# A two-layer diffusion step on one core: ten weight slots before the first expert choice, split constants, attention weights read early

## The chip, the core and the metric

The kernel runs on one NeuronCore of a Trainium2 chip. The metric is the device time of one execution in microseconds, as the median of several runs. In the text TensorE is PE, VectorE is DVE, ScalarE is ACT, GpSimd is POOL and SyncE is SP. SyncE does nothing but issue direct DMAs, in the order of its list; GpSimd issues the gathers.

## The reference, cut to what matters

Two groups of tokens (128 of a prompt, 512 of a sample) pass through two layers with shared weights. One layer, in float32 throughout:

```python
mod = silu(cond) @ w_ada[l] + b_ada[l]                 # shift1, scale1, gate1, shift2, scale2, gate2
h = rmsnorm(x, norm_mix) * (1 + scale1) + shift1
proj = h @ w_in[l]                                     # 3232 columns
hg = rmsnorm(scan_forward + scan_backward) * silu(gate)        # 8 heads, gated linear recurrence
ckv = rmsnorm(ckv_raw); k, v = ckv @ mla_wkvb[l]; q = rmsnorm(cq) @ mla_wqb[l]
attn = softmax(q k) v                                  # 8 heads; the sample also sees the cached context
x = x + gate1 * (concat(hg, attn) @ w_out[l])
h2 = rmsnorm(x, norm_ffn) * (1 + scale2) + shift2
q = h2 @ peer_wq[l]                                    # 2048 columns; scores against 2 x 128 keys per head
idx = top 16 of 16 x 16 candidates, for each of 8 heads       # 128 experts of 16384 per token
x = x + gate2 * sum(softmax(best) * gelu(h2 . u[idx]) * v[idx])
```

Outputs are the final norm of both groups and the prompt's new caches and scan states.

## The kernel before

The work is cut into four passes `p` = (group, layer): 0 is the prompt's first layer (one tile of 128 tokens), 1 the sample's first (four tiles), 2 and 3 the same for the second layer. Ten token tiles `u` = 0 to 9 in all need 128 gathers of `peer_u` rows and 128 of `peer_v` rows each; a gather brings one row of 4 KB for each of 128 tokens, 512 KB.

`plan()` makes one list of steps, `PLAN`. Every engine walks this same list in order and does its own part of each step; semaphores tie the parts together. Where two lists are merged, `spread(a, b)` gives each step a place by its cost: the middle of its cost in its list over the list's total, and sorts by that. `spread_pairs` counts every step as 3. The steps that matter here are `ada` (one 128-column tile of the modulation, 48 for a layer), `norm`, `inp` (one tile of w_in, 26), `hg` (a level of the scan), `latn`, `latT`, `kn` and `va` (latent norm, its transposes, keys and values of attention), `q`, `sc`, `pv` (attention), `outp` (two tiles of w_out), `wq` (two tiles of w_q), `score`, `topk` (the choice for one head), `u` and `v` (two gathered rows each).

SyncE issues, for each step, the weight tiles that it uses (512 KB each, from `WEIGHTS`), `n % WR` of three slots in `wring`; it waits until the tile three before is used. `wb` reads the attention weights `wkvb` and `wqb` (1024 and 1152 KB), `keys` reads the sub-keys into the same SBUF as `wkvb`, and both wait in the queue for whoever still uses that SBUF; all that stands behind them in SyncE's list waits too. The nine constants, x among them (2560 KB), are issued first, on one semaphore that TensorE, ScalarE and VectorE wait for in full.

GpSimd fills a ring of ten slots, `ring`, with gathered rows; VectorE takes the dot products with u rows (L1556) and TensorE sums v rows (L972). The first gather needs the first `topk`, at the end of pass 0's query projection. The steps up to there have 90 weight tiles: 48 `ada`, 26 `inp`, 8 of w_out and 8 of w_q. Their order is 16 `ada`, `norm`, 26 `inp`, the scan with 8 `ada` among it, then attention with 24 `ada`, then output projection, `norm`, query projection.

A modulation tile is 8 matmuls with a 32-column stationary operand (L950, 16 records), an eviction by ScalarE, and a small matmul that turns it into columns (L942), which VectorE adds to the bias (L1596). `norm` squares x on VectorE (L1269), waits for ScalarE's root, scales (L1281), and then TensorE transposes (L721) and ScalarE evicts with scale and shift (L1032). In pass 0 the scan's buffers QP, KX, P and X lie over `wqb` and `wkvb`. That is why `wb` waits for the scan's end.

## Time and profile before

| what | value |
|---|---|
| median of 3 runs | 4698.39 us (4684.86 to 4701.82) |
| span of the profiled execution | 5196.0 us |
| PE, DVE, POOL, ACT busy | 2947.7, 2863.5, 2429.0, 607.1 us |
| gathers | 2560, 1342.34 MB, 68.6% of 16 engines' span |
| direct reads and writes | 240.76 MB, 13.3% |
| HBM read | 1579.47 MB |

The profiled execution is one execution, and its page gives no time beside its span; it is longer than the timed runs. The busy times overlap each other. A DMA share of 1 means that all 16 DMA engines had packets all the time.

### The profile page before, as it was taken

Reading aid. Unit: us, or ns where it says so; the run is one execution under the profiler, and the core shown is the slowest. Engines: PE = TensorE matmul, PEld = TensorE weight load, DVE = VectorE, ACT = ScalarE, POOL = GpSimd, SP = SyncE. Lnnn points to the kernel's source line nnn. Section 1 sums busy time; section 2 is a strip of 40 time slices with the busy share of each in tenths; the row PEclk is TensorE's granted clock in tenths of the full one; section 3 lists DMA queues with packets and bytes.
Section 4 is the critical chain, followed back from the end, with each engine's and each line's share of the span. In section 5 each row is a group of like instructions: output and inputs, shape, how many; then the busy total and the mean of one; then the engine's idle time right before and its main releaser. Section 6 shows DMA issues by size and latency. Waiting matters only on the chain. (4 is left out here: it accounts for less than half of the span.)

```text
span 5196.0 us, 51262 instructions
## 1 busy us (share of the span) xinstructions
PE 2947.7 (57%) x18894; PEld 1865.7 (36%) x18894; DVE 2863.5 (55%) x7112; ACT 607.1 (12%) x1305; POOL 2429.0 (47%) x2565
## 2 busy tenths in 40 slices
PE   6758667744677576237457643685466467025025
PEld 5545633634435453123136333253432353000000
DVE  1258572289247544776863458326935833873740
ACT  2210121210111011110101110211111110000000
POOL 0024154045354435555653643445446646566665
PEclk9579788656885698568678875786677577556556
DMA  6468477278899879899985987788789989899998
GB/s 213 147 232 337 148 267 269 92 277 333 312 382 360 303 266 367 345 360 369 348 343 195 335 329 243 259 333 326 301 319 359 358 306 361 326 359 366 363 373 330
DMA packets 440728, 1586.38 MB, mean 305 GB/s; under 512 B 54560, under 2 KB 56992, under 8 KB 438688
## 3 DMA queue, kind: packets, MB, share of 16 engines
q0 software_dynamic: 368640, 1342.34, 68.6%
q1 hardware_dynamic: 71840, 240.76, 13.3%
q8 instruction: 152, 2.49, 0.2%
q14 instruction: 96, 0.79, 0.0%
HBM read 1579.47 MB, written 3.44 MB: 305 GB/s over the span
## 5 line engine op out<-in xcount | busy, mean ns | idle before, releaser
L679 POOL DMA_INDIRECT ring<-in_peer_u,eidx x1280 | 1206.6, 943 | 1581.2 <-DVE dot L1556 780.4
L679 POOL DMA_INDIRECT ring<-in_peer_v,eidxT x1280 | 1222.0, 955 | 1162.7 <-PE acc L972 624.1
L1556 DVE CUSTOM_DVE_ANT_0 ring<-ring,acc 128x1024 f32<-128x1024 f32 x1280 | 1487.5, 1217 | 99.5 <-issue 68.8
L972 PE MATMUL acc<-ring,wz 128*32 128x512 f32 x5120 | 872.3, 771 | 356.4 <-DMA ring<-in_peer_v,eidxT 269.0
L972 PEld LDWEIGHTS acc<-ring,wz 128*32 128x32 f32 x5120 | 145.4, 123 | 858.7 <-issue 833.1
L926 PE MATMUL pp<-hT,wring 128*128 128x128 f32 x2560 | 352.5, 295 | 138.1 <-issue 97.0
L926 PEld LDWEIGHTS pp<-hT,wring 128*128 128x128 f32 x2560 | 329.6, 208 | 177.3 <-issue 124.3
L757 PE MATMUL pp<-hT,wring 128*128 128x128 f32 (+2 forms) x960 | 245.2, 419 | 147.8 <-issue 122.1
L763 PE MATMUL pp<-wring,hT 128*128 128x128 f32 (+1 forms) x2240 | 276.2, 284 | 40.2 <-issue 22.5
L763 PEld LDWEIGHTS pp<-wring,hT 128*128 128x128 f32 x2240 | 267.6, 199 | 59.7 <-issue 36.0
L721 PE MATMUL tb<-ident,gl 128*128 128x128 f32 x10 | 4.5, 446 | 436.7 <-DVE gl L1563 409.6
L757 PEld LDWEIGHTS pp<-hT,wring 128*128 128x128 f32 x960 | 157.0, 214 | 245.0 <-issue 213.0
L922 PE MATMUL pp<-wring,hT 128*128 128x128 f32 x1280 | 181.2, 303 | 84.3 <-issue 48.0
L1496 DVE MAX8 v<-lat 128x8 f32<-128x128 f32 x160 | 46.9, 293 | 307.7 <-ACT lat L1012 263.1
L922 PEld LDWEIGHTS pp<-wring,hT 128*128 128x128 f32 x1280 | 171.0, 215 | 99.0 <-issue 59.5
L892 PE MATMUL tb<-U,hT 128*128 128x64 f32 x480 | 101.8, 388 | 163.7 <-ACT hT L1012 128.1
L721 PE MATMUL tb<-ident,xn 128*128 128x128 f32 (+1 forms) x240 | 52.9, 393 | 241.4 <-DVE xn L1281 173.6
L786 PE MATMUL pp<-wqb 64*128 64x128 f32 x1120 | 113.1, 351 | 120.4 <-DVE wqb L1326 97.9
L1291 DVE TENSOR_SCALAR U<-U,omlb,lb 128x128 f32<-128x128 f32 (+2 forms) x40 | 13.4, 409 | 275.2 <-ACT lat L1012 275.2
L721 PEld LDWEIGHTS tb<-ident,gl 128*128 128x128 f32 x10 | 1.7, 174 | 438.9 <-DVE gl L1563 411.2
L786 PEld LDWEIGHTS pp<-wqb 64*128 64x128 f32 x1120 | 96.2, 246 | 174.1 <-issue 171.5
L892 PEld LDWEIGHTS tb<-U,hT 128*128 128x128 f32 x480 | 93.3, 293 | 179.7 <-ACT hT L1012 140.7
(207 smaller groups left out, 3597.9 us busy)
## 6 DMA issues: line engine op xcount, KB each, us to landing
wring<-in_w_q SPq DMA_DIRECT2D x128, 512.0 KB
wring<-in_w_in SPq DMA_DIRECT2D x125, 512.0 KB
wring<-in_w_ada SPq DMA_DIRECT2D x96, 512.0 KB
wring<-in_w_out SPq DMA_DIRECT2D x64, 512.0 KB
ring<-in_peer_u,eidx POOLq DMA_INDIRECT x1280
ring<-in_peer_v,eidxT POOLq DMA_INDIRECT x1280
wkvb<-in_keys SPq DMA_DIRECT2D x5, 1024.0 KB
wqb<-in_wqb SPq DMA_DIRECT2D x4, 1152.0 KB
```

What stands on the lines that cost most here:

```text
L679: pool.indirect_dma_start(ring[:, n % GR, :], None, A[table], bass.IndirectOffsetOnAxis(ap=rows, axis=0),).then_inc(s_g[n % GR], 16)
L721: ins = nc.tensor.transpose(tb[0:m, n % 2, i * P:(i + 1) * P], piece, ident[:, :])
L757: ins = nc.tensor.matmul(out[:, 0:n], wt[:, c, :], h[:, c, 0:n], start=(c == 0), stop=(c == KC - 1))
L763: ins = nc.tensor.matmul(out[:, (t - t0) * P:(t - t0) * P + m], h[:, c, (t - t0) * P:(t - t0 + 1) * P], wt[:, c, 0:m], start=(c == 0), sto ...
L786: ins = nc.tensor.matmul(out[:, e * 512 + gg * P:e * 512 + (gg + 1) * P], KX[r, m % 2, gg, :], QP[r, m % 2, gg, :], start=True, stop=True)
L892: ins = nc.tensor.matmul(tb[:, bank, 256:256 + DK], cols[:, hi, a, :], vatt[:, a, hh * DK:(hh + 1) * DK], start=(a == 0), stop=(a == kt_n ...
L922: project_chunk(p, t, i, "id", lambda out, w, m, c: nc.tensor.matmul(out, m, w, start=(c == 0), stop=(c == KC - 1)))
L926: project_chunk(p, t, i, "ia", lambda out, w, m, c: nc.tensor.matmul(out, w, m, start=(c == 0), stop=(c == KC - 1)))
L972: ins = nc.tensor.matmul(acc[32 * q:32 * q + 32, half * 512:(half + 1) * 512], wz[:, at:at + 32], row[:, half * 512:(half + 1) * 512], sta ...
L1291: ins = v.tensor_scalar(f, f, omlb[:, d, l, a:a + 1], lb[:, d, l, a:a + 1], ALU.mult, ALU.add)
L1496: link(v.max(vals[:, 0:8], src))
L1556: v.tensor_tensor_reduce(rows, rows, acc[:, :], 1.0, 0.0, ALU.mult, ALU.add, dot[:, n:n + 1])\
```

## The change

Before the first `score` step, weight tiles go round ten slots: the three of `wring` and seven of the gather ring, which nobody fills yet. The first gather then waits for that step's matmuls. After it three slots are used as before. The constants are read in parts: five small ones first, x of the prompt tile after four modulation tiles, the rest after six tiles of w_in. The mask cast moves to `fgate`. In pass 0 the scan's buffers, the latents' transposes, the gain rows and the probabilities lie elsewhere, so the attention weights are read amid the projection and the stores of caches and state are issued after attention. `norm` is divided into `rms` (VectorE, and ScalarE's root) and `norm` (TensorE, and ScalarE's evictions); in pass 0 `rms` stands after the twelfth modulation tile. The keys' read waits for the last values or score step instead of all steps ahead of it, and pass 0's stands right after the values.

The core of the diff (left out: where code only takes the new homes in place of the old):

```diff
@@ -34,6 +34,7 @@
 N_ADA, SECT = 48, 8
 WR = 3
 GR = 10
+WE = 10
 CU = 2
 CV = 2
 WG = 16
@@ -74,7 +75,10 @@
 
 def norms(p, b):
 
-    return [(("norm", p, t, 0), 8) for t in range(*BATCHES[p][b])]
+    out = []
+    for t in range(*BATCHES[p][b]):
+        out += [(("rms", p, t, 0), 4), (("norm", p, t, 0), 4)]
+    return out
 
 
 def projections(p, b, lo=0, hi=N_IN):
@@ -96,7 +100,7 @@
 def keys_values(p):
 
     nt, g = NT[p], PASSES[p][0]
-    out = [(("wb", p), 0)]
+    out = [(("wb", p), 0), (("stores", p), 0)] if p else []
     if g:
         out += [(("hgS", p), 5)] + [(("hgo", p, t), 2) for t in range(nt)]
     return out + [(("latT", p), 3 * nt), (("kn", p), 20 if g else 6), (("va", p), 9 if g else 2)]
@@ -125,7 +129,8 @@
 def joined(p, t):
 
     tiles = served(p, t)
-    return [(("outp", p, t, i), 5 * len(tiles)) for i in range(N_OUT // WCH)] + [(("norm", p, a, 1), 10) for a in tiles]
+    return [(("outp", p, t, i), 5 * len(tiles)) for i in range(N_OUT // WCH)] \
+        + [step for a in tiles for step in ((("rms", p, a, 1), 4), (("norm", p, a, 1), 6))]
 
 
 def searched(p, t):
@@ -188,10 +193,15 @@
     def alone(steps):
         return [step for step, _ in steps]
 
-    out = alone(modulations(0, 0, 2 * SECT) + norms(0, 0) + projections(0, 0))
+    first = modulations(0, 0, 2 * SECT)
+    rms, norm = norms(0, 0)
+    inputs = projections(0, 0)
+    out = alone(first[:4] + [(("x0",), 0)] + first[4:12] + [rms] + first[12:] + [norm] + inputs[:6]
+                + [(("rest",), 0)] + inputs[6:12] + [(("wb", 0), 0)] + inputs[12:])
     out += spread(scans(0, 0, 1), modulations(0, 2 * SECT, 3 * SECT))
-    out += spread(keys_values(0) + spread_pairs(attention(0, 0), outputs(0)), modulations(0, 3 * SECT, N_ADA))
-    out += alone([(("keys", 0), 0)] + opened(0))
+    out += spread(keys_values(0) + [(("keys", 0), 0)] + spread_pairs(attention(0, 0), outputs(0)),
+                  modulations(0, 3 * SECT, N_ADA))
+    out += alone([(("stores", 0), 0)] + opened(0))
     entry = {0: (0, 0, norms(1, 0) + projections(1, 0, 0, 20)), 1: (1, 0, attention(1, 1) + joined(1, 1)), 6: (3, 0, attention(3, 1) + joined(3, 1))}
     ahead = {1: spread_pairs(attention(1, 0), outputs(1)) + [(("keys", 1), 0)] + opened(1)}
     prompt_q = queries(2, 0)
...
@@ -255,7 +265,9 @@
         return {"mods": 1}
     if name == "norm":
         n = 4 if a[2] else 2
-        return {"ms": 1, "rt": 1, "xn": 1, "tp": n, "te": n}
+        return {"tp": n, "te": n}
+    if name == "rms":
+        return {"ms": 1, "rt": 1, "xn": 1}
     if name == "inp":
         return {"it": 1, "ia": 1}
     if name == "hg":
...
@@ -380,6 +392,23 @@
 
 
 WEIGHTS = weight_tiles()
+EARLY = sum(k < PLACE["score", 0, 0, 0] for _, _, _, k in WEIGHTS)
+
+
+def weight_slots():
+
+    slots, turns, olds, last, count = [], [], [], {}, {}
+    for n in range(len(WEIGHTS)):
+        slot = n % WE if n < EARLY else n % WR
+        count[slot] = count.get(slot, 0) + 1
+        slots.append(slot)
+        turns.append(count[slot])
+        olds.append(last.get(slot))
+        last[slot] = n
+    return slots, turns, olds
+
+
+W_SLOT, W_TURN, W_OLD = weight_slots()
 GATHERS = gathers()
 GATHER_AT = {}
 for _n, _x in enumerate(GATHERS):
...
@@ -444,7 +469,12 @@
         qn = xn[:, 256:1024]
         KTn = xn[:, :].rearrange("p (d g t) -> p d g t", d=2, t=P)
         ring = sb("ring", [P, GR, D])
+        cqT0 = ring[:, GR - 1, 0:QL].rearrange("p (c t) -> p c t", t=P)
+        ckvT0 = ring[:, GR - 1, QL:QL + KVL].rearrange("p (c t) -> p c t", t=P)
+        P0 = ring[:, GR - 2, 0:256].rearrange("p (b k) -> p b k", b=2)
+        PT0 = ring[:, GR - 2, 256:512].rearrange("p (b a t) -> p b a t", b=2, t=P)
         h2 = sb("h2", [P, 2, D])
+        staged = h2[:, 0, 0:6 * P].bitcast(I32)
         wz = sb("wz", [P, 2 * 32 * WG + 32])
         wvT = sb("wvT", [P, P])
         S = sb("S", [P, 2, 4, DK])
...
@@ -501,12 +529,14 @@
 
 
         s_const = sem("s_const")
+        s_x0 = sem("s_x0")
+        s_rest = sem("s_rest")
         s_cond = sem("s_cond")
         s_zero = sem("s_zero")
         s_row = sem("s_row")
         s_lbd = sem("s_lbd")
         s_lbe = sem("s_lbe")
-        s_w = [sem(f"s_w{i}") for i in range(WR)]
+        s_w = [sem(f"s_w{i}") for i in range(WE)]
         s_sw = sem("s_sw")
         s_wb = sem("s_wb")
         s_keys = sem("s_keys")
@@ -558,14 +588,37 @@
         )}
 
         consts = [(ident[:, :], A["ident"]), (cond[:, :, :], A["cond"]), (bada[:, :, :], A["b_ada"]),
-                  (nrm[:, :, :, :], A["nrm"]), (lbl[:, :, :, :], A["lbl"]), (x[:, :, :], A["x"]),
-                  (U[:, 0:6 * P].bitcast(I32).rearrange("p (d m t) -> p d m t", d=2, t=P), A["masks"]),
-                  (rope[:, :, :, :], A["rope"]), (hrow[:, :, :], A["hrow"])]
+                  (nrm[:, :, :, :], A["nrm"]), (lbl[:, :, :, :], A["lbl"])]
+        rest = [(staged.rearrange("p (d m t) -> p d m t", d=2, t=P), A["masks"]), (x[:, 1:5, :], A["x"][:, 1:5, :]),
+                (rope[:, :, :, :], A["rope"]), (hrow[:, :, :], A["hrow"])]
         CONST = 16 * len(consts)
 
-        def probabilities(t):
-
-            return (Pn1, PT1) if t else (Pn, PT)
+        def weight_slot(n):
+
+            return wring[:, W_SLOT[n]] if W_SLOT[n] < WR else \
+                ring[:, W_SLOT[n] - WR, :].rearrange("p (c n) -> p c n", n=P)
+
+        def scan_home(p):
+
+            if p:
+                flat = wqbf[:, 0:1024], wqbf[:, 1024:2048], wkvb[:, 0, :], wkvb[:, 1, :]
+            else:
+                flat = [b[:, 1:3, :].rearrange("p a b -> p (a b)") for b in (V, GT, o)] + [h2[:, 1, :]]
+            return [f.rearrange("p (d g t) -> p d g t", d=2, t=P) for f in flat]
+
+        def gain_rows(p):
+
+            if p:
+                return hflat[:, 2048:2048 + QL], hflat[:, 2048 + QL:2048 + QL + KVL]
+            return V[:, 3, 0:QL], GT[:, 3, 0:KVL]
+
+        def latents_home(p):
+
+            return (cqT, ckvT) if p else (cqT0, ckvT0)
+
+        def probabilities(p, t):
+
+            return (Pn1, PT1) if t else (Pn, PT) if p else (P0, PT0)
 
         def normed_home(p, t):
 
...
@@ -606,16 +659,21 @@
                 name, a = step[0], step[1:]
                 while n < len(WEIGHTS) and WEIGHTS[n][3] == k:
                     array, index, _, _ = WEIGHTS[n]
-                    if n >= WR:
-                        which, value = WEIGHTS[n - WR][2]
+                    if W_OLD[n] is not None:
+                        which, value = WEIGHTS[W_OLD[n]][2]
                         sp.wait_ge(C[which], value)
                     src = A[array]
                     for i in index:
                         src = src[i]
-                    dst = wring[:, n % WR, :, 0:src.shape[2]] if src.shape[2] < P else wring[:, n % WR]
-                    sp.dma_start(dst, src).then_inc(s_w[n % WR], 16)
+                    dst = weight_slot(n)[:, :, 0:src.shape[2]] if src.shape[2] < P else weight_slot(n)
+                    sp.dma_start(dst, src).then_inc(s_w[W_SLOT[n]], 16)
                     n += 1
-                if name == "small":
+                if name == "x0":
+                    sp.dma_start(x[:, 0, :], A["x"][:, 0, :]).then_inc(s_x0, 16)
+                elif name == "rest":
+                    for dst, src in rest:
+                        sp.dma_start(dst, src).then_inc(s_rest, 16)
+                elif name == "small":
                     p, = a
                     g, l = PASSES[p]
                     if g:
@@ -627,15 +685,21 @@
                         sp.dma_start(S[:, :, :, :], A["state"][l]).then_inc(s_sw, 16)
                 elif name == "rows":
                     p, = a
-                    sp.wait_ge(C["it"], after(("inp", p, len(BATCHES[p]) - 1, N_IN - 1), "it"))
-                    sp.dma_start(qrow[:, :], A["qrow"][PASSES[p][1]]).then_inc(s_row, 16)
-                    sp.dma_start(kvrow[:, :], A["kvrow"][PASSES[p][1]]).then_inc(s_row, 16)
+                    if p:
+                        sp.wait_ge(C["it"], after(("inp", p, len(BATCHES[p]) - 1, N_IN - 1), "it"))
+                    qrow, kvrow = gain_rows(p)
+                    sp.dma_start(qrow, A["qrow"][PASSES[p][1]]).then_inc(s_row, 16)
+                    sp.dma_start(kvrow, A["kvrow"][PASSES[p][1]]).then_inc(s_row, 16)
                 elif name == "wb":
                     p, = a
                     g, l = PASSES[p]
-                    sp.wait_ge(C["it"], after(("hg", p, NT[p] - 1, LV - 1), "it"))
+                    if p:
+                        sp.wait_ge(C["it"], after(("hg", p, NT[p] - 1, LV - 1), "it"))
                     sp.dma_start(wkvb[:, :, :], A["wkvb"][l]).then_inc(s_wb, 16)
                     sp.dma_start(wqb[:, :, :], A["wqb"][l]).then_inc(s_wb, 16)
+                elif name == "stores":
+                    p, = a
+                    g, l = PASSES[p]
                     if not g:
                         sp.wait_ge(C["ia"], after(("hg", p, 0, LV - 1), "ia"))
                         sp.dma_start(O["state"][l], Uc[:, :, 0, :].rearrange("p d (g n) -> p d g n", n=DK))\
@@ -644,7 +708,8 @@
                         sp.dma_start(O["ckv"][l], ckv[:, 0, :]).then_inc(s_out, 16)
                         sp.dma_start(O["kpe"][l], kpe[:, 0, :]).then_inc(s_out, 16)
                 elif name == "keys":
-                    sp.wait_ge(C["it"], before(k, "it"))
+                    last = max(i for i in range(k) if PLAN[i][0] in ("va", "score"))
+                    sp.wait_ge(C["it"], before(last + 1, "it"))
                     sp.dma_start(keysT, A["keys"][PASSES[a[0]][1]]).then_inc(s_keys, 16)
                 elif name == "y":
                     i = a[0] - (NU - 5)
@@ -673,6 +738,8 @@
                     rows = eidxT[:, u % 3, token(col):token(col) + 1]
                     if col == 0:
                         pool.wait_ge(C["te"], after(("soft", u), "te"))
+                if n == 0:
+                    pool.wait_ge(C["it"], after(("score", 0, 0, 0), "it"))
                 if n >= GR:
                     which, value = GATHERS[n - GR][3]
                     pool.wait_ge(C[which], value)
...
@@ -696,9 +763,9 @@
 
             def wtile():
                 nonlocal wn
-                pe.wait_ge(s_w[wn % WR], 16 * (wn // WR + 1))
+                pe.wait_ge(s_w[W_SLOT[wn]], 16 * W_TURN[wn])
                 wn += 1
-                return wring[:, (wn - 1) % WR]
+                return weight_slot(wn - 1)
 
             def pair(by):
 
@@ -736,7 +803,7 @@
                 ins.then_inc(C["it"], 1)
 
             def norm(k, p, t, which):
-                pe.wait_ge(C["xn"], before(k, "xn") + 1)
+                pe.wait_ge(C["xn"], before(k, "xn"))
                 for i in range(2):
                     transposes([xn[:, (4 * i + c) * P:(4 * i + c + 1) * P] for c in range(4)])
                 if which:
...
@@ -1015,11 +1085,15 @@
                 act.wait_ge(C["ms"], before(k, "ms") + 1)
                 nc.scalar.activation(dst, src, ACT.Sqrt).then_inc(C["rt"], 1)
 
+            def norm_root(k, p, t, which):
+                root(k, st[:, 2:3], st[:, 1:2])
+
             def norm(k, p, t, which):
                 g, l = PASSES[p]
                 if t == 0:
                     act.wait_ge(C["mods"], after(("adafin", l, which), "mods"))
-                root(k, st[:, 2:3], st[:, 1:2])
+                    if p == 1 and not which:
+                        act.wait_ge(s_Sst, 16)
                 n = before(k, "tp")
                 for i in range(2):
                     src = got_t(n + i)
...
+                if p == 2:
+                    act.wait_ge(s_Sst, 16 * 2)
+                turned_q, turned_kv = latents_home(p)
                 for t in range(NT[p]):
-                    copy(cqT[:, :, t * P:(t + 1) * P], got_t(n)[:, 0:3, :]).then_inc(C["te"], 1)
+                    copy(turned_q[:, :, t * P:(t + 1) * P], got_t(n)[:, 0:3, :]).then_inc(C["te"], 1)
                     n += 1
...
+                if hh == 0 and p:
                     act.wait_ge(s_out, 32 * (PASSES[p][1] + 1))
                 act.wait_ge(C["mx"], before(k, "mx") + 1)
                 u = U0[p] + t
                 if u:
                     act.wait_ge(C["td"], H * (u - 1) + hh + 1)
-                nc.scalar.activation(probabilities(t)[0][:, hh % 2, 0:keys], b[:, 0:keys], ACT.Exp, scale=SCALE, bias=nb[:, hh % 2, :],
+                nc.scalar.activation(probabilities(p, t)[0][:, hh % 2, 0:keys], b[:, 0:keys], ACT.Exp, scale=SCALE, bias=nb[:, hh % 2, :],
                                      accum_out=es[:, hh:hh + 1]).then_inc(C["ia"], 1)
 
...
@@ -1184,6 +1260,8 @@
             def sub_key_scores(k, p, t, i):
                 if t:
                     act.wait_ge(C["eh"], after(("soft", U0[p] + t - 1), "eh"))
+                if p == 0:
+                    act.wait_ge(s_out, 32)
                 b = got_pair(before(k, "it"))
                 copy(SS[:, 8 * i:8 * i + 8, :], b.rearrange("p (a k) -> p a k", k=NK)).then_inc(C["ia"], 1)
 
...
@@ -1271,8 +1349,10 @@
                 dve.wait_ge(C["rt"], before(k, "rt") + 1)
                 link(v.reciprocal(s[:, 3:4], s[:, 2:3]))
 
-            def norm(k, p, t, which):
+            def normed(k, p, t, which):
                 g = PASSES[p][0]
+                if p == 0 and not which:
+                    dve.wait_ge(s_x0, 16)
                 if before(k, "tp"):
                     dve.wait_ge(C["tp"], before(k, "tp"))
                 if not which and t == BATCHES[p][-1][0] > 0:
@@ -1284,6 +1364,9 @@
 
                 g, l = PASSES[p]
                 t0, t1 = BATCHES[p][b]
+                if p == 0:
+                    dve.wait_ge(s_rest, 16 * len(rest))
+                    link(v.tensor_copy(mk[:, :, :], staged.rearrange("p (m t) -> p m t", t=P)))
                 dve.wait_ge(C["ia"], before(k, "ia"))
                 for d in range(2):
                     for a in range(4):
...
@@ -1422,6 +1506,7 @@
                 g, nt = PASSES[p][0], NT[p]
                 dve.wait_ge(s_sw, 16 * n_small(p))
                 dve.wait_ge(s_row, 32 * (p + 1))
+                qrow, kvrow = gain_rows(p)
                 link(v.memset(st8[:, 1, :], 1.0))
                 for t in range(nt):
                     link(v.tensor_tensor_reduce(xn[:, 0:QL], cq[:, t, :], cq[:, t, :], 1.0 / QL, EPS, ALU.mult, ALU.add,
```

## Rows read from the trace of the kernel before

**Rows 1.** Timeline, GpSimd, 300 to 420 us: start, length, what, wait before it.

```profile
320.55 1.09 POOL L679 DMA_INDIRECT ring<-in_peer_u,eidx  x1 [319.57 <-DVE eidx L1533]
```

**Rows 2.** Windows: busy us of each engine, granted clock, DMA share, GB/s.

```profile
14.00:46.00 32.00, 25.44 (x288) 17.80 (x288) 4.65 (x29) 5.58 (x18) 0.00 (x0) 1.00 0.85 276
...
54.40:112.30 57.90, 52.78 (x416) 49.79 (x416) 0.00 (x0) 9.53 (x28) 0.00 (x0) 1.00 0.66 203
...
121.00:168.00 47.00, 36.53 (x344) 30.59 (x344) 30.74 (x62) 6.09 (x16) 0.00 (x0) 0.54 0.19 56
...
194.10:254.00 59.90, 48.53 (x424) 33.11 (x424) 13.56 (x62) 17.63 (x52) 0.00 (x0) 0.59 0.52 157
...
320.30:5196.00 4875.70, 2716.41 (x16909) 1672.98 (x16907) 2790.80 (x6885) 541.12 (x1138) 2428.61 (x2560) 0.71 0.84 313
```

**Rows 3.** Waits of TensorE, 0 to 320 us: total us, times, longest.

```profile
PE pp L950 <- DMA wring<-in_w_ada: 30.9, 11, 14.8
...
PE pp L763 <- DMA wring<-in_w_in: 3.3, 7, 0.9
...
PE pp L926 <- DMA wring<-in_w_q: 2.2, 3, 1.5
...
PE pp L757 <- DMA wring<-in_w_in: 1.5, 3, 0.6
...
PE pp L922 <- DMA wring<-in_w_out: 1.1, 2, 0.7
```

**Rows 4.** Timeline, 0 to 60 us, the start.

```profile
3.08 0.43 SPq L603 DMA_DIRECT2D x<-in_x  x1
...
13.41 0.22 ACT L1242 ACTIVATE cond<-cond 128x16 f32<-128x16 f32 x1 [9.68 <-DMA hrow<-in_hrow]
...
14.80 2.27 PE L950 MATMUL pp<-wring,cond 128*32 128x128 f32 x32 [14.80 <-DMA wring<-in_w_ada]
```

**Rows 5.** DMA, 0 to 60 us in 40 slices of 1.5 us.

```profile
GB/s 0 73 244 164 437 437 437 297 408 421 320 180 325 320 276 227 224 377 238 300 188 240 257 363 328 183 221 328 333 251 161 268 36 0 0 0 0 0 0 87
```

**Rows 6.** Timeline, 0 to 60 us, modulation end and norm.

```profile
37.14 1.08 PE L950 MATMUL pp<-wring,cond 128*32 128x128 f32 x16
...
38.73 1.08 PE L950 MATMUL pp<-wring,cond 128*32 128x128 f32 x16
...
44.63 1.12 PE L942 MATMUL pp<-pick,hT 128*128 128x2 f32 x4
...
50.31 1.97 PE L721 MATMUL tb<-ident,xn 128*128 128x128 f32 x8 [4.56 <-DVE xn L1281]
...
54.41 5.75 PE L757 MATMUL pp<-hT,wring 128*128 128x128 f32 x32 [2.14 <-ACT hT L1032]
```

**Rows 7.** Timeline, VectorE, 105 to 200 us.

```profile
116.10 0.07 DVE L1425 MEMSET st<- 128x8 f32 x1 [0.74 <-DMA hT<-in_kvrow]
```

**Rows 8.** Timeline, the DMA queue of SyncE, and TensorE behind it.

```profile
168.00 0.33 SPq L637 DMA_DIRECT2D wkvb<-in_wkvb  x1
...
171.00 73.89 SPq L616 DMA_DIRECT2D wring<-in_w_ada  x24
...
253.83 0.33 SPq L648 DMA_DIRECT2D wkvb<-in_keys  x1
...
178.70 1.08 PE L950 MATMUL pp<-wring,cond 128*32 128x128 f32 x16 [10.73 <-DMA wring<-in_w_ada]
```

**Rows 9.** Timeline, TensorE, 105 to 200 us.

```profile
190.02 0.65 PE L950 MATMUL pp<-wring,cond 128*32 128x128 f32 x16
...
194.09 0.64 PE L950 MATMUL pp<-wring,cond 128*32 128x128 f32 x16
...
195.15 4.12 PE L861 MATMUL pp<-wqb,hT 128*128 128x384 f32 x12
```

**Rows 10.** TensorE at a later norm, and what ended the idle time ahead of L1272.

```profile
1729.80 1.97 PE L721 MATMUL tb<-ident,xn 128*128 128x128 f32 x8 [10.56 <-DVE xn L1281]
...
  ACT st L1016: 12.0, 19
```

37 lines of the change are left out of this document (16 added, 21 removed).

## The prediction

> **What bounds the kernel now.** I read the windows first, to see which stretches wait for what. The change says "before the first choice", so the first number is where that choice lies: the first gather is issued at 320.55 us [rows 1]. After it the span has 4876 us with the DMA engines 84% busy, and before it no stretch but one is near that [rows 2]. So there are two regimes: a tail in which 2560 gathers of 128 rows and the weights share the DMA engines, and a head of 320 us in which TensorE walks alone through modulation, input projection, scan, attention, output and query projection. Only the head is edited; the tail starts when the head ends, so a microsecond taken from the head should be a microsecond of the whole. The head's length is then the question, and the second view is whom TensorE waited for in it [rows 3]: 30.9 us for adaLN weights, 4.8 for w_in, 2.2 for w_q, 1.1 for w_out. Together that is 39 us, the most that any depth of weight slots can give directly. The third view, the timeline, says which waits these are; I take the parts in order of time.
>
> **Part 1, constants in two parts: 7.5 us.** TensorE's first matmul is at 14.80, released by a DMA. The activation that waits for all constants ran only at 13.41, since x (2.5 MB) is issued at 3.08, ahead of the weights [rows 4]. The slices of 1.5 us show that data flows at full rate (437 GB/s) from about 6 us on, some 3 us after that issue [rows 5]. Now five small constants go first and the first weight tile takes x's place at 3.08: it lands at about 6.0 + 0.52 MB / 437 GB/s = 7.2. I take a first matmul at 7.3; by the same rows it could be 6.0 to 8.5. The gain is 7.5 (6.3 to 8.8). What waits behind the later half (masks cast, x of the other tiles, rope) is needed at 112 us or later; 2.6 MB is 6 us of transfer and lies beside w_in's matmuls.
>
> **Part 2, ten slots in the modulation stretch: 3.4 us.** From 14.80 to 45.75 there are 16 tiles (80% busy [rows 2]). Two tiles without a wait are 1.59 apart (37.14 and 38.73), the last ends at 45.75 [rows 6]. All waits there are 30.9 - 14.8 (the start) - 10.7 (part 5) = 5.4 us. At 437 GB/s a tile takes 1.2 us, under 1.59, so with ten slots TensorE is the bound and the 5.4 goes. Against it stands the RMS step, now after the twelfth tile: squares on VectorE, a root on ScalarE with its table load, scaling on VectorE, the whole of which took 4.56 us where TensorE waited for it [rows 6], and the next tiles' evictions queue behind it on both. TensorE has at most two tiles (2 x 1.59, less what the first eviction holds) in hand meanwhile, so I charge 2.0 (0 to 3). Net 3.4.
>
> **Part 3, RMS ahead of the last tiles: 4.6 us.** From the last modulation matmul's end (45.75) to the first projection (54.41) are 8.66 us. The transposes waited 4.56 for the scaled rows [rows 6]. That row is now long done; what is left is 50.31 to 54.41, 4.1 us of transposes and evictions. Gain 4.6 (4.0 if ScalarE has to wait for Am, the two small steps after the last column).
>
> **Part 4, projection: 4.8 us, and 0.7.** 57.9 us with TensorE busy 52.8 [rows 2]; the waits for w_in are 3.3 + 1.5 [rows 3]. A tile takes about 2 us of TensorE and 1.2 of DMA, so they go. Its demand with the moved reads is 13.2 + 2.6 + 2.2 MB, 41 us at the rate above, and ten tiles of it are already read. Moving the gain rows' read up removes the 0.74 that VectorE waited for kvrow [rows 7]. The scan is bound by VectorE and ScalarE (DMA 19% busy, no wait for weights) [rows 2]: nothing there. Its other homes for QP, KX, P and X have the same sizes: nothing.
>
> **Part 5, attention weights early: 10.7 us.** At 168.00 the queue may at last issue wkvb and wqb, then three stores, and only at 171.00 the next weight tile; TensorE stands 10.73 us until 178.70 [rows 8]. With these read during the projection and the stores moved behind attention, the tile is there. All 10.7 goes.
>
> **Part 6, the keys' read moved forward: a new wait, -6.3 us.** This is the part that speaks against the change. Today it stands after attention (253.83) and its wait is behind all work [rows 8]. In the new order its place is computed from the weights given to spread: keys at 11/65 = 0.169 of its list, adaLN tile 28 at 6.75/37 = 0.182, values at 0.154. So the queue must issue keys (which waits for the values' matmuls, because they share wkvb) before tile 28, and every slot of the ring is useless for tiles from 28 on until then. TensorE's next instruction after the values is exactly tile 28 (194.09) [rows 9]. It must wait for the queue to wake, for 1.05 MB of keys and for 0.52 MB of the tile. The near row is part 5's stall: 10.7 us for 3.15 MB, of which 7.2 is transfer and 3.5 the rest, 3 of that in issues of several DMAs. For 1.57 MB that makes 3.6 + 0.8 at the least and 3.6 + 3.5 at the most; I take 6.3 (4.4 to 7.1), since the start of the flow after an issue took near 3 us in part 1. The Trainium skill, DMA: Bandwidth & Descriptors, section on the anatomy of one DMA, says that a DMA engine never waits on a semaphore, the issuing sequencer does, and gives 2.0 us fixed plus bytes over 436 GB/s; its price here would be 5.6 us, and the sum 0.7 us better. No row shows this stall, only part 5's.
>
> Behind it, the clock. In the rows the 16 small matmuls of a tile take 0.65 us at 190.02, after dense matmuls, and 1.08 at 178.70, after standing idle [rows 9]; these are the levels of 2.4 and 1.2 GHz. The fast stretch covers the query projection too (12 matmuls in 4.12 us). An idle gap of 6 us in the middle puts that part on the lower level: up to 4.1 + 3 tiles x 0.65 = 6 us, part of it returned when the clock rises again later. I take 3 (0 to 6).
>
> **Part 7, output and query projection: 3.2 us.** The waits for w_out and w_q are 1.1 + 2.2 [rows 3]; the last eight w_q tiles have three slots again, so I leave 0.1.
>
> **Part 8, RMS split from norm everywhere, keys' waits relaxed later.** VectorE's RMS now comes a few steps before TensorE's transposes. In the stretches of dots TensorE's wait is cover anyway. In the three norms that lie among value sums (one is at 1729.80, 10.56 us of wait [rows 10]) TensorE can take one or two sums in between. 0 to 10 us; I take 3. The keys' relaxed waits in the three later passes let w_out's first tiles be read sooner. The same wait stands in the head today, and all waits for w_out behind it are 1.1 us [rows 3], so I cost them at nothing (at most 3 x 1.1).
>
> **Sum.** 7.5 + 3.4 + 4.6 + 4.8 + 0.7 + 10.7 - 6.3 - 3 + 3.2 = 25.6 in the head, 28.6 with part 8. The profiled execution shows 5196.0 us of span and nothing around it; the median of the runs is 4698.4, 498 less. The head has few DMA packets and is bound by TensorE, so I take its microseconds over unscaled: 4698.4 - 28.6 = **4670**. The first gather would be at 320.6 - 25 = 295.5 in a profile.
>
> **Rivals.** *The keys' wait costs little* (the clock rises in the now unbroken stretch before it, or the modulation stretch reaches the upper level too, where a tile is bound by 1.2 us of DMA: 6 us more): head 35 to 41, about 4660. For it: TensorE is denser everywhere. Against: from 194 to 254 it was busy 81% with such matmuls, and the granted clock was 0.59 of full, mostly the lower level [rows 2]. Chance 0.15. *The tail doesn't take the gain over*: a DMA share of 84% on average [rows 2] leaves stretches that other waits set, and a changed step order may lose 10 to 25 us there; half or less arrives, about 4688. For it: 94% of the time lies there and step order changes in it. Chance 0.20. *Slower*: the split RMS. VectorE stands in each RMS until ScalarE takes the root, and while it stands no gather slot comes free. The rows give 12.0 us for this in 19 of them [rows 10]. If ScalarE, reached earlier in its order, is still behind an eviction, each of the 18 outside the first stretch pays more; it needs 1.5 us each to cancel 26, and 2.8 us each for +23.5: about 4722. Against it: ScalarE's own list has the same order. Chance 0.09. The forecast's own mechanism has 0.56; a net under 23.5 us within it 0.11.
>
> **Numbers.** 0.5% is 23.5 us, about what a measurement can tell from no change. Faster by over 0.5%: 0.45 + 0.15 = 0.60. Within: 0.11 + 0.20 = 0.31. Slower: 0.09. The bounds of the parts give gains from 19 to 51; the likeliest case has 4650 to 4682. To hold 8 in 10 the range takes in most of the second rival, and the runs of before differ by 17 us among themselves: 4645 to 4696.
>
> **What would show it.** First matmul at 7.3; first projection at 39; scan's first matmul at 99.5; no DMA wait at the scan's end; an idle gap of about 6 us at adaLN tile 28, with keys issued just before it; first gather near 295. If the gap is missing, part 6 is wrong and the time is near 4660; if the head is right and the time isn't, it was the tail.

## The result: 4634 us, faster than the range allowed

The changed kernel takes 4634.3 us (4629.2 to 4640.4, four runs), beside 4695.8 for the one before; the ratio is 0.9879, interval 0.9861 to 0.9897. I had forecast 4670 with a range from 4645 to 4696: the sign was right, the size was half. The gain is about 57 us by the ratio and 61 by the medians, where I had 29. Two later comparisons of the same two kernels gave ratios of 0.9887 (0.9859 to 0.9916) and 0.987 (0.9839 to 0.9901).

One thing about the profile that I had worked from: it was no ordinary execution of the kernel before. The timed runs of that kernel fall into two groups by chip: 4663 to 4713 us on the chips numbered 9 and 13 and in the result above, 5187 to 5224 us on 8 and 12. Its span of 5196 us puts the old profile into the second group; which chip it came from is not on record. Experiments 5 to 12 ran on the slower chips, the others on the faster ones, so all kernels are compared by their ratio to the kernel before that ran beside them. The head, which is the part up to the first gather, is nearly the same in both groups (first gather at 320.6 and 318.2 us); the tail behind it is not.

The profile of the changed kernel, first TensorE's waits up to the first gather, to be read beside [rows 3]:

```profile
PE pp L1020 <- DMA wring<-in_w_ada: 7.1, 1, 7.1
...
PE pp L1020 <- DMA ring<-in_w_ada: 6.4, 2, 6.1
...
PE pp L996 <- DMA wring<-in_w_q: 0.5, 1, 0.5
```

The waits for w_in and w_out are gone, w_q has half a microsecond left, and of the adaLN waits three remain: the first tile and two on ring slots. The timeline has them in place. The start, as in [rows 4]; x now goes into the queue at 4.98, behind four tiles, and the first matmul is at 7.13:

```profile
3.08 1.38 SPq L669 DMA_DIRECT2D wring<-in_w_ada  x3
...
4.98 0.59 SPq L672 DMA_DIRECT2D x<-in_x  x1
...
7.13 2.25 PE L1020 MATMUL pp<-wring,cond 128*32 128x128 f32 x32 [7.13 <-DMA wring<-in_w_ada]
```

The DMA slices of 1.5 us, as in [rows 5]. The rate stays near its top through the whole stretch; in the kernel before it fell after 15 us, to 276 GB/s between 14 and 46 us:

```profile
GB/s 0 78 65 248 399 418 415 429 412 426 421 412 429 407 415 429 407 429 412 421 412 410 421 507 421 426 361 399 426 418 401 440 434 436 416 410 413 418 421 431
```

The end of modulation and the projection, as in [rows 6]. The one wait that the early RMS causes is the 0.51 at 27.70 (ScalarE's eviction ran at 27.29, behind the table load and the root of the RMS), the transposes follow the last column without a gap, and the last group of w_in ends at 86.18:

```profile
27.70 1.08 PE L1020 MATMUL pp<-ring,cond 128*32 128x128 f32 x16 [0.51 <-ACT hT L1082]
...
32.79 1.95 PE L788 MATMUL tb<-ident,xn 128*128 128x128 f32 x8
...
36.94 10.01 PE L824 MATMUL pp<-hT,ring 128*128 128x128 f32 x64 [2.20 <-ACT hT L1106]
...
82.52 3.66 PE L830 MATMUL pp<-wring,hT 128*128 128x128 f32 x32
```

The scan's end, as in [rows 8] and [rows 9]. The tile at 138.84 waits for nothing, and the new wait of part 6 stands at 159.74. The keys' read is issued at 153.64, just as the values' matmuls end (151.63 + 1.98), and the tiles behind it in SyncE's list follow at 154.01:

```profile
153.64 0.33 SPq L713 DMA_DIRECT2D wkvb<-in_keys  x1
...
154.01 3.09 SPq L669 DMA_DIRECT2D ring<-in_w_ada  x6
...
138.84 1.08 PE L1020 MATMUL pp<-wring,cond 128*32 128x128 f32 x16
...
151.63 1.98 PE L922 MATMUL pp<-wkvb,ring 128*128 128x512 f32 x4
...
159.74 1.08 PE L1020 MATMUL pp<-ring,cond 128*32 128x128 f32 x16 [6.12 <-DMA ring<-in_w_ada]
...
161.21 6.14 PE L931 MATMUL pp<-wqb,ring 128*128 128x384 f32 x12
```

The first gather, as in [rows 1]:

```profile
283.92 1.08 POOL L746 DMA_INDIRECT ring<-in_peer_u,eidx  x1 [282.94 <-DVE eidx L1618]
```

And the windows, as in [rows 2] (projection, scan, attention, tail). In the projection TensorE is now busy 98% of the time instead of 91%, with the DMA engines at 0.96 instead of 0.66:

```profile
7.00:33.00 26.00, 24.99 (x289) 18.61 (x290) 5.19 (x25) 5.82 (x18) 0.00 (x0) 1.00 1.02 417
...
36.90:87.00 50.10, 49.23 (x416) 49.12 (x416) 1.04 (x3) 10.28 (x29) 0.00 (x0) 1.00 0.96 367
...
94.00:138.80 44.80, 32.86 (x344) 27.35 (x344) 30.83 (x62) 6.12 (x17) 0.00 (x0) 0.61 0.07 24
...
157.00:221.00 64.00, 49.75 (x422) 33.42 (x422) 13.38 (x61) 16.95 (x51) 0.00 (x0) 0.59 0.74 250
...
284.00:4631.50 4347.50, 2610.11 (x16904) 1615.24 (x16903) 2806.66 (x6884) 541.01 (x1138) 2438.24 (x2560) 0.74 0.90 352
```

### The profile page after: what moved, and what is told of

It reads as the page before. It is cut to its first block and busy times, and to the rows that moved or that the text cites. A ratio compares the mean times of both kernels' runs of the same rounds, so it can differ in the third digit from the quotient of the medians.

```text
span 4631.5 us, 51264 instructions
## 1 busy us (share of the span) xinstructions
PE 2834.6 (61%) x18894; PEld 1805.8 (39%) x18894; DVE 2879.4 (62%) x7112; ACT 606.8 (13%) x1305; POOL 2438.7 (53%) x2565
## 5 line engine op out<-in xcount | busy, mean ns | idle before, releaser
L1641 DVE CUSTOM_DVE_ANT_0 ring<-ring,acc 128x1024 f32<-128x1024 f32 x1280 | 1505.1, 1217 | 142.4 <-DMA ring<-in_peer_u,eidx 123.1
L1042 PE MATMUL acc<-ring,wz 128*32 128x512 f32 x5120 | 846.9, 756 | 384.8 <-DMA ring<-in_peer_v,eidxT 372.3
L996 PE MATMUL pp<-hT,wring 128*128 128x128 f32 x2448 | 312.0, 289 | 51.0 <-DMA wring<-in_w_q 49.6
L996 PEld LDWEIGHTS pp<-hT,wring 128*128 128x128 f32 x2448 | 299.1, 203 | 82.4 <-DMA wring<-in_w_q 56.0
L830 PE MATMUL pp<-wring,hT 128*128 128x128 f32 (+1 forms) x2096 | 258.5, 286 | 33.8 <-DMA wring<-in_w_in_tail 20.2
L830 PEld LDWEIGHTS pp<-wring,hT 128*128 128x128 f32 x2096 | 253.3, 203 | 49.1 <-DMA wring<-in_w_in_tail 21.5
L824 PE MATMUL pp<-hT,wring 128*128 128x128 f32 (+2 forms) x816 | 209.3, 418 | 16.0 <-DMA wring<-in_w_in 9.6
L788 PE MATMUL tb<-ident,xn 128*128 128x128 f32 (+1 forms) x240 | 52.3, 390 | 219.0 <-DVE xn L1361 176.0
L824 PEld LDWEIGHTS pp<-hT,wring 128*128 128x128 f32 x816 | 130.1, 202 | 104.1 <-issue 61.0
L992 PE MATMUL pp<-wring,hT 128*128 128x128 f32 x1184 | 151.9, 292 | 27.4 <-DMA wring<-in_w_out 19.9
L992 PEld LDWEIGHTS pp<-wring,hT 128*128 128x128 f32 x1184 | 146.6, 206 | 37.2 <-DMA wring<-in_w_out 22.9
L854 PE MATMUL pp<-wqb 64*128 64x128 f32 x1008 | 93.3, 337 | 93.8 <-DVE wqb L1410 93.8
L946 PE MATMUL pp<-U,hT 96*128 96x128 f32 (+1 forms) x288 | 143.9, 643 | 4.2 <-ACT hT L1082 4.1
```

The costliest lines, as they stand in the source:

```text
L788: ins = nc.tensor.transpose(tb[0:m, n % 2, i * P:(i + 1) * P], piece, ident[:, :])
L824: ins = nc.tensor.matmul(out[:, 0:n], wt[:, c, :], h[:, c, 0:n], start=(c == 0), stop=(c == KC - 1))
L830: ins = nc.tensor.matmul(out[:, (t - t0) * P:(t - t0) * P + m], h[:, c, (t - t0) * P:(t - t0 + 1) * P], wt[:, c, 0:m], start=(c == 0), sto ...
L854: ins = nc.tensor.matmul(out[:, e * 512 + gg * P:e * 512 + (gg + 1) * P], KX[r, m % 2, gg, :], QP[r, m % 2, gg, :], start=True, stop=True)
L946: ins = nc.tensor.matmul(b[:, k0:k0 + kn], QT[0:DQ, hh, :], kT[0:DQ, hh, k0:k0 + kn], start=True, stop=True)
L992: project_chunk(p, t, i, "id", lambda out, w, m, c: nc.tensor.matmul(out, m, w, start=(c == 0), stop=(c == KC - 1)))
```

## The experiments

Thirteen of the sixteen experiments were timed in several runs beside the kernel before; three (1, 9, 10) are single executions, for their traces. The marks that I use from the traces are the first gather (end of the head) and the moment at which ScalarE first copies a tile's rows into `acc` (start of tile u).

**1. The kernel before, once more.** No edit.

> The kernel before, profiled once more, unchanged. The profile used for the prediction spans 5196 us where the timed runs are 4698; this one should span about 4690. Theory A (the head gives 36 to 37 us, the rest of the 61 us comes from edits of the tail): the first gather is again at about 320 us and the first dot product 18 us behind it or less. Theory B (the head's gain is larger than the two first profiles show, since one of them was disturbed): the first gather or the first dot product is later than in the first profile, by 10 us or more.

The timeline, TensorE and GpSimd:

```profile
54.00 6.25 PE L757 MATMUL pp<-hT,wring 128*128 128x128 f32 x39 [2.14 <-ACT hT L1032]
...
119.21 3.51 PE L777 MATMUL pp<-U 64*128 64x128 f32 x32 [7.82 <-ACT wkvb L1080]
...
175.19 1.08 PE L950 MATMUL pp<-wring,cond 128*32 128x128 f32 x16 [11.12 <-DMA wring<-in_w_ada]
...
191.27 4.12 PE L861 MATMUL pp<-wqb,hT 128*128 128x384 f32 x12
...
249.78 3.76 PE L734 MATMUL pp<-ident,mods 128*128 128x128 f32 x16
...
318.22 1.08 POOL L679 DMA_INDIRECT ring<-in_peer_u,eidx  x1 [317.24 <-DVE eidx L1533]
```

The window over its tail, beside the last one of [rows 2]:

```profile
318.00:4694.10 4376.10, 2617.43 (x16906) 1619.87 (x16904) 2806.56 (x6885) 540.86 (x1138) 2434.05 (x2560) 0.74 0.89 349
```

The span is 4694.1, the first gather at 318.22 and the first dot product at 329.3, where the old profile has 339.1. So the old profile's head was off by 2 us, and its first dot product came 7 us later still behind the first gather. That belongs to the chip: the distance from the first gather to the first dot product is 11 to 12 us in all nine profiles of the faster chips and 16.5 to 18.6 us in all nine of the slower ones. Against this profile the head's gain is 318.2 - 283.9 = 34.3 us (theory A, though a little under its 36 to 37), and I take it as the left side of the account further down. It is good to some 2 us: with the changed head the first gather stands between 281.7 and 285.5 in nine profiles.

**2. The head's edits alone.** Order of all steps after the first choice as before:

```diff
-        out += [(("rms", p, t, 0), 4), (("norm", p, t, 0), 4)]
+        out += [(("rn", p, t, 0), 8)] if p else [(("rms", p, t, 0), 4), (("norm", p, t, 0), 4)]
...
-    + [step for a in tiles for step in ((("rms", p, a, 1), 4), (("norm", p, a, 1), 6))]
+    + [(("rn", p, a, 1), 10) for a in tiles]          # "rn" becomes rms, norm side by side at the end
...
-                    sp.wait_ge(C["it"], before(last + 1, "it"))
+                    sp.wait_ge(C["it"], before(k if k > PLACE["score", 0, 0, 0] else last + 1, "it"))
...
-                5: norms(3, 1) + projections(3, 1) + scans(3, 3, 4) + keys_values(3)[:6],
+                5: norms(3, 1) + projections(3, 1) + scans(3, 3, 4) + keys_values(3)[:7],
```

> The changed kernel with the order of all steps after the first choice put back to that of before (rms and norm adjacent and placed as one step, keys' reads behind all work again from the second on, the last hgo step back in its list). Only the head's edits are left. Theory A (two parts: head 37 us, tail's order 25 us): 4658 (4650 to 4665). Theory B (all of it is the head): 4634 within 6.

4645.0 us (4640.2 to 4673.3), ratio 0.9915 (0.9886 to 0.9944): 40 us of gain. That lies between the two theories (4650 to 4665, and 4628 to 4640) and bears out neither. Beside it the changed kernel again (**4**) had 4638.2 (4631.8 to 4641.0), ratio 0.9887.

> The changed kernel unchanged, beside the others on one chip: 4634 within 6, ratio 0.987 to 0.989.

The two intervals overlap, so this pair alone doesn't prove that the tail's order does anything. It bounds the head's part: by its interval, 26 to 53 us.

**3. Keys' read behind attention.**

```diff
-    out += spread(keys_values(0) + [(("keys", 0), 0)] + spread_pairs(attention(0, 0), outputs(0)),
+    out += spread(keys_values(0) + spread_pairs(attention(0, 0), outputs(0)),
...
-    out += alone([(("stores", 0), 0)] + opened(0))
+    out += alone([(("keys", 0), 0), (("stores", 0), 0)] + opened(0))
```

> The changed kernel with one step moved: the keys' read of pass 0 stands behind attention, not right after the values. Its relaxed wait stays. The stall of 6.1 us ahead of modulation tile 28 goes, and the query projection is in the fast clock: by the rows 8 us less, 4626 (4622 to 4630). Rival: the tail (bound by gathers) gives the 8 us back, 4634 within 3.

The timeline, TensorE and GpSimd:

```profile
151.64 1.99 PE L922 MATMUL pp<-wkvb,ring 128*128 128x512 f32 x4
...
154.62 4.12 PE L931 MATMUL pp<-wqb,ring 128*128 128x384 f32 x12
...
275.31 1.09 POOL L746 DMA_INDIRECT ring<-in_peer_u,eidx  x1 [274.33 <-DVE eidx L1618]
```

In the head all came as expected. The stall is gone, the query projection is back at 4.12 us for its 12 matmuls, where the changed kernel had 6.14, and the first gather is 8.6 us sooner. The time was 4633.8 (4625.7 to 4643.2), ratio 0.9889, against 4638.2 and 0.9887 of the changed kernel: outside the 4622 to 4630 expected, and at the number of the rival.

**12 and 16. The same once more, on a slower and a faster chip.**

> The kernel with the keys' read of pass 0 behind attention, once more. Head: first gather 8 us ahead of the changed kernel's 282 to 284. Time: 0.987 of before (8 us or 0.17% under the changed kernel's 0.9887) if the tail carries it; 0.9887 if not. Both lie within one interval; the marks of each tile's start are to say where it is lost.

> Keys' read behind attention. The head gives 8 us; if they arrive, 6 to 10 us faster than e13. If the gathers take them back, within 3 us.

First gather at 273.7 and 274.2; 5145.0 us, ratio 0.9877 (0.9859 to 0.9895), on the slower chip, and 4636.1 (4617.8 to 4642.2), ratio 0.9883 (0.9853 to 0.9913), on the faster, where the changed kernel beside it had 4629.2. So in three comparisons the 8 us are plain in every trace up to the first gather, and in the time they are not shown: by the medians once 4 us better, once 7 worse, with intervals of some 14 us to either side (experiment 12 has no changed kernel beside it). It is no version that beats the changed one by a measurement.

**5. The tail's edits alone.** All of the head back in the old order with three slots (left out: the attention weights wait for the scan again, and the first keys' read for all steps ahead of it):

```diff
-WE = 10
+WE = 3
...
-    out = alone(first[:4] + [(("x0",), 0)] + first[4:12] + [rms] + first[12:] + [norm] + inputs[:6]
-                + [(("rest",), 0)] + inputs[6:12] + [(("wb", 0), 0)] + inputs[12:])
+    out = alone([(("x0",), 0), (("rest",), 0)] + first + [rms, norm] + inputs)
...
-    out += spread(keys_values(0) + [(("keys", 0), 0)] + spread_pairs(attention(0, 0), outputs(0)),
+    out += spread([(("wb", 0), 0), (("stores", 0), 0)] + keys_values(0) + spread_pairs(attention(0, 0), outputs(0)),
...
-    out += alone([(("stores", 0), 0)] + opened(0))
+    out += alone([(("keys", 0), 0)] + opened(0))
```

> The changed kernel with every edit of the head put back in order and number of slots (all constants ahead of the weights, three slots, attention weights and stores behind the scan, keys behind attention, rms next to norm); only the order of steps and the keys' waits after the first choice are the changed ones. Theory A (the tail's order gives 7 to 25 us by itself): 4663 to 4678, and the first gather at 318. Theory B (the tail's gain in the first pair of profiles was scatter between executions): 4685 within 4, ratio 0.998 to 1.002.

First gather at 316.2, nearly as before, and yet the ratio is 0.9958 (0.994 to 0.9976): 5177.5 against 5199.6, 22 us there, which is 20 at the faster chips' length (11 to 28 by the interval). Theory A: the tail's edits do pay, by themselves, and my forecast for them was 3 us.

**6 and 7. Which of the tail's two edits.** The same edits as in experiment 2, one at a time: in 6 rms and norm are one step again, in 7 only the keys' waits are the old ones.

> The changed kernel with rms and norm put back together after the first choice, placed as one step as before; keys' waits stay relaxed. If the split is what the tail gains by: 4645 (as the kernel with the head alone), the dots of u = 3 and 5 start 5 to 15 us later. If not: 4638 within 4.

> The changed kernel with the keys' reads after the first choice waiting for all steps ahead of them again; the split stays. If the relaxed waits are what the tail gains by: 4645. If not: 4638 within 4; I expected nothing of them in the prediction.

6 had 0.9905 (0.9885 to 0.9925), 7 had 0.989 (0.9863 to 0.9916). The old waits for keys show no cost against the changed kernel's 0.987 to 0.989 (no changed kernel ran beside them). For the split, 11 us between 6 and 7 with overlapping intervals were a hint, not more.

**11. The split undone in another way.** Each rms moved to right before its norm, all other steps in the changed order:

```diff
-    return out + [("y", NU - 1)]
+    out.append(("y", NU - 1))
+    later = {step for step in out if step[0] == "rms" and (step[1] or step[3])}
+    out = [step for step in out if step not in later]
+    return [s for step in out
+            for s in ([("rms",) + step[1:], step] if step[0] == "norm" and ("rms",) + step[1:] in later else [step])]
```

> The changed kernel with each rms after the first one moved to right before its norm; all other steps keep the changed order. If VectorE's early rms is what the split gains: about 0.991 of before (as the unsplit tail on its chip, 0.9905). If the gain is the shifted order of the other steps (a topk and the value sums a place earlier): 0.989, as the changed kernel.

0.9926 (0.991 to 0.9943), against 0.9877 (0.9859 to 0.9895) for experiment 12 beside it, which has the early rms and differs otherwise only in one read of the head: 27 us, with the intervals apart. So the shifted order of the other steps brings nothing by itself (with the split undone in full it was 0.9905); what pays is VectorE's early rms.

**13 to 15. All three side by side.**

> The changed kernel as the reference of this call: 0.988 to 0.989 of before.

> The unsplit tail beside it. If the early rms gives the tail's gain: 8 to 15 us slower than e13. If it was scatter: within 4 us of it.

> rms moved to right before norm, changed order otherwise. Early rms: 8 to 20 us slower than e13, level with e14 or a little behind it. Shifted order: level with e13.

| kernel | median us (runs) | ratio to before |
|---|---|---|
| changed | 4629.2 (4624.4 to 4651.9) | 0.987 (0.9839 to 0.9901) |
| split undone | 4651.4 (4639.4 to 4658.5) | 0.9921 (0.9896 to 0.9947) |
| rms beside norm | 4661.4 (4655.5 to 4669.6) | 0.9941 (0.992 to 0.9963) |

The differences are 22 and 32 us, both larger than the 8 to 15 and 8 to 20 expected. The second is clear of the changed kernel's interval, so with experiment 11 the early rms is shown to pay. The first overlaps it at the edge; three comparisons have it in the same direction, at 22 us here, 11 (6 against 7) and 7 (2 against 4, in which the keys' waits and one `hgo` step differ too). TensorE's wait for the scaled rows, summed over the execution, and its waits at the norms among the dots of tile 1 and of tile 6, in the three kernels in this order:

```profile
PE tb L788 <- DVE xn L1361: 181.7, 18, 33.7
...
1157.98 1.97 PE L788 MATMUL tb<-ident,xn 128*128 128x128 f32 x8 [18.06 <-DVE xn L1361]
...
3350.19 1.97 PE L788 MATMUL tb<-ident,xn 128*128 128x128 f32 x8 [20.02 <-DVE xn L1361]
```

```profile
PE tb L789 <- DVE xn L1362: 214.2, 19, 36.9
...
1158.61 1.97 PE L789 MATMUL tb<-ident,xn 128*128 128x128 f32 x8 [24.35 <-DVE xn L1362]
...
3341.41 1.97 PE L789 MATMUL tb<-ident,xn 128*128 128x128 f32 x8 [22.31 <-DVE xn L1362]
```

```profile
PE tb L792 <- DVE xn L1365: 224.6, 19, 36.7
...
1172.79 1.97 PE L792 MATMUL tb<-ident,xn 128*128 128x128 f32 x8 [32.35 <-DVE xn L1365]
...
3371.49 1.97 PE L792 MATMUL tb<-ident,xn 128*128 128x128 f32 x8 [32.27 <-DVE xn L1365]
```

The early rms takes 33 and 43 us off the sums, and the sums repeat. On the faster chips they are 176.0 to 181.7 us in five profiles with the early rms, 206.2 and 214.2 with the split undone and 218.7 in the kernel before; on the slower chips 143 to 154 in six profiles, against 174.1 with the split undone, 193.6 with rms moved and 173.6 before. At each of these two norms the changed list has rms, two steps of dots, a choice step, norm. With the split undone the choice stands behind both, with rms moved it stands ahead of both, and TensorE waits for the choice as well as for the rows: the longest of the three waits.

The span of one profile may be trusted less here. The profiled execution of the changed kernel was the slowest of its five (4651.9), and that of the split undone nearly its fastest (4641.1). By the two spans alone I would have read the opposite.

**8. Three slots, all other edits kept.**

```diff
-WE = 10
+WE = 3
```

> The changed kernel with three weight slots before the first choice, all else as changed. By the prediction's parts 2, 4 and 7 the ten slots are worth 5.4 + 4.8 + 3.2 = 13 us; by the two profiles the projection alone took 8 us less, so 17: first gather at 299 to 301, time 4652 to 4655. The stall behind the keys' read should stay near 6 us, since the slots don't help there.

The timeline, TensorE and GpSimd:

```profile
64.29 11.95 PE L824 MATMUL pp<-hT,wring 128*128 128x128 f32 x80 [5.54 <-DMA wring<-in_w_in]
...
84.12 12.12 PE L830 MATMUL pp<-wring,hT 128*128 128x128 f32 x80 [4.71 <-DMA wring<-in_w_in]
...
314.56 1.09 POOL L746 DMA_INDIRECT ring<-in_peer_u,eidx  x1 [313.57 <-DVE eidx L1618]
```

I missed this one, and it is the most instructive run. First gather at 314.6, not 300, ratio 0.996 (0.9942 to 0.9979), level with the tail's edits alone (0.9958): without the slots nearly all of the head's gain is gone. The two waits above are the later half of the constants (5.54 us) and the attention weights (4.71), which now stand in the middle of a weight stream with three tiles in hand. The stall behind the keys' read was 6.05 us, as expected. So the reads moved forward are worth what they are only with the ten slots. Ten slots with none of the reads moved were not run.

**9 and 10. The other two parts, one execution each.** 9 issues x and the rest of the constants first again, 10 puts the attention weights' read back behind the scan (left out: its removal from the projection, and the wait for the scan that it gets again):

```diff
-    out = alone(first[:4] + [(("x0",), 0)] + first[4:12] + [rms] + first[12:] + [norm] + inputs[:6]
-                + [(("rest",), 0)] + inputs[6:12] + [(("wb", 0), 0)] + inputs[12:])
+    out = alone([(("x0",), 0), (("rest",), 0)] + first[:12] + [rms] + first[12:] + [norm]       # 9
+                + inputs[:12] + [(("wb", 0), 0)] + inputs[12:])
...
+    out += spread([(("wb", 0), 0)] + keys_values(0) + [(("keys", 0), 0)] + ...                  # 10
```

> The changed kernel with x, masks, rope and hrow issued right after the small constants, ahead of all weight tiles; ten slots and all else as changed. Read in the head: if reading them first cost the old kernel 7.7 us, the first matmul is at 14.8 again instead of 7.1 and the first gather 7 to 8 us later than with the changed kernel (291 to 292). Rival: with ten slots behind it the later start is caught up in the projection, since the tiles are DMA-late only at the start: the first gather 3 us later or less.

> The changed kernel with the attention weights' read back behind the scan's last matmul (their SBUF is free, the wait is put there on purpose); the stores stay behind attention. Part 5 of the prediction: a DMA wait of 8 to 9 us at the scan's end (2.7 MB, no stores ahead), and the stall behind the keys' read stays near 6; first gather at 291 to 293. Rival: the ten slots hide it, first gather at 284, because the modulation tiles next in the list are read and only keys and values wait.

The timeline of 9:

```profile
14.77 2.27 PE L1020 MATMUL pp<-wring,cond 128*32 128x128 f32 x32 [14.77 <-DMA wring<-in_w_ada]
...
293.08 1.08 POOL L746 DMA_INDIRECT ring<-in_peer_u,eidx  x1 [292.10 <-DVE eidx L1618]
```

The timeline of 10:

```profile
148.62 1.08 PE L1020 MATMUL pp<-wring,cond 128*32 128x128 f32 x16 [8.96 <-DMA wring<-in_w_ada]
...
292.19 1.08 POOL L746 DMA_INDIRECT ring<-in_peer_u,eidx  x1 [291.21 <-DVE eidx L1618]
```

9 starts at 14.77, 7.6 us behind the changed kernel, and has its first gather at 293.1, 9.2 behind. The late start is not caught up: from the first matmul to the keys' stall TensorE waits for no DMA in this trace, so tiles that are read still earlier have nothing to give back. 10 waits 8.96 us at the scan's end and has its first gather at 292.2, 8.3 behind. With some 2 us of scatter in this mark both rivals (3 us or less, and none) are out.

## Why the prediction was wrong, point by point

The step that failed is first of all part 8, the price of the tail's order, and next to it part 4, the projection. The account by marks is taken from the profile of experiment 1 and that of the changed kernel, both of the faster group; predicted shifts in brackets:

| mark | before, us | changed, us | gained up to there | this part (predicted) |
|---|---|---|---|---|
| first matmul | 14.81 | 7.13 | 7.7 | 7.7 (7.5) |
| first projection | 54.00 | 36.94 | 17.1 | 9.4 (8.0) |
| scan's first matmul | 119.21 | 94.07 | 25.1 | 8.1 (5.5) |
| tile at the scan's end | 175.19 | 138.84 | 36.4 | 11.2 (10.7) |
| query projection | 191.27 | 161.21 | 30.1 | -6.3 (-6.3) |
| gate row of output | 249.78 | 221.21 | 28.6 | -1.5 (-3, for the clock) |
| first gather | 318.22 | 283.92 | 34.3 | 5.7 (3.2) |
| end of the span | 4694.1 | 4631.5 | 62.6 | 28.3 (3) |

- **Part 1** right, to 0.2 us.
- **Part 2, oversized cost.** I charged 2.0 us for the RMS amid modulation; it took 0.51. Only one eviction came late by it, and TensorE had one more tile's matmuls to do meanwhile.
- **Part 3** right: 4.1 us from transposes to projection, and no wait for Am.
- **Part 4, undersized.** I counted only TensorE's waits for w_in, 4.8 us, and took 52.8 us of busy time as fixed, so 53.1 us were to be left. It took 49.2 in all (36.94 to 86.18). The busy time was not fixed: a tile between two waits takes 2.05 us in the trace of before, one in an unbroken run 1.8 (seven in 12.67 in the changed kernel's). Each of ten or eleven waits cost its own length and some 0.25 us of overlap between tiles, by this estimate 3 us. I take the same for part 7, where 5.7 came for 3.2, but no run isolates it.
- **Part 5** right.
- **Part 6** right, and it was the step I was least sure of: 6.12 us of wait at tile 28, predicted 6.3 from the place of two steps in a sorted list (that the account shows exactly -6.3 is chance: 6.12 of wait and 0.2 of small shifts at the lower clock). The issuing queue does the waiting: nothing is issued between 101 and 153.64, and then the keys and six tiles in 3.5 us. The Trainium skill (DMA: Bandwidth & Descriptors, Anatomy of one DMA) says that a semaphore wait happens on the issuing sequencer, and the trace agrees. The price in the same section of the Trainium skill, 2.0 us and the bytes over 436 GB/s, is given for DMAs issued by GpSimd; the estimate by it, 5.6 us, is half a microsecond under this stall of SyncE's queue. The clock fell as said: the granted clock reads 0.50 from 159.7 to 161.2 us, behind the stall, and 1.00 from 167.4, the query projection took 6.14 us instead of 4.12, and at 170.07 a modulation tile took 0.64 us again. Experiment 3, without the stall, has the gate row at 212.59 instead of 221.21: 8.6 us for stall and clock together, so 2.5 for the clock, where I had 3.
- **Part 8 failed.** The steps that failed were "In the stretches of dots TensorE's wait is cover anyway" and "0 to 10 us; I take 3". Measured were 20 us for the tail's edits alone (experiment 5), 22, 11 and 7 for the split undone, and 27 and 32 for rms moved to its norm with the rest of the order kept. I had also misread my row: the norm at 1729.80 [rows 10] lies not among value sums but among the dots of tile 2, and the changed kernel waits 10.56 us at it as before. TensorE's waits in the traces of experiments 13 to 15 go like this:

| norms | changed, us | split undone, us | rms moved, us |
|---|---|---|---|
| among the dots of tiles 1 and 6 | 38.1 | 46.7 | 64.6 |
| three among value sums | 8.6 | 24.2 | 12.9 |
| all others | 135.0 | 143.4 | 147.1 |

  So the early rms shortens waits of both kinds. That those among dots are not mere cover is indicated by the last two columns: with rms moved TensorE waits 11 us less among value sums and 18 more at two norms among dots, and the kernel is 10 us slower than with the split undone (11 by the ratios of 11 and 6; the intervals overlap in both pairs). How much each norm pays in time isn't settled: single executions differ by more than the parts. Of the 28.3 us in the account, 24 lie between the marks of tiles 5 and 6, where the one profile of the kernel before has 525 us and the faster chips' eight profiles with ten slots have 502 to 514, whatever the order, so this line of the account says little of the split.
- **Carry-over.** The head's microseconds arrive as far as the intervals tell: 34 at the first gather, 40 timed with the head alone (26 to 53), 37 with the split undone (44 by the ratio of experiment 6). The rival that the tail would take over half or less is out, except for the last 8 of the moved keys' read, which stay unproved. On the way some are lost and found: with the head alone the shift was 34 us at tile 0 and 30 at tile 1 (28 to 31 in five profiles of the faster chips with the same head, 26 with rms moved); the cause is open. The kernel with the moved keys' read lost 7.6 of its 43 there (5.9 of 44 in experiment 16).
- **Of the range.** It was built from bounds on parts, and two of these bounds were no bounds: busy time as fixed, and the split as nothing among dots. The sums had slips too: the parts' upper bounds add to 47, not 51 (which takes the keys' stall at nothing), and 320.6 - 25.6 is 295.0, not 295.5. Either way the measured 57 to 61 lies outside. The forecast also rested on one profile of a chip 11% slower than the one that was timed; in the head that did little harm (2 us), and from the tail I took one row, the misread one.
- **A step that I overlooked.** `keys_values(3)[:6]` is a slice, and the added stores step moves one `hgo` step from the dots of tile 5 to its value sums. Undone in experiment 2, kept in 5, 6, 11, 14 and 15; it was not measured by itself.

## What to carry to other kernels

TensorE's waits cost more than their length here: some 0.25 us each in the projection on top. Where a stretch has many short waits, count the start of the next group as well, so that removing n waits is worth their sum plus n times that refill. A read moved forward needs depth in the stream that it is put into; test the two together, since one alone can lose what both gain. When a step is split between engines, ask for each place where it is put what stands behind it on the waiting engine, and don't write off a wait because another engine is the bound of that stretch; and before a tail of a few per cent is read from one profile of each kernel, see whether the profiled executions are typical of their runs.
